# A pair of gate/up tiles, 2 of its 8 pairs of k tiles by seven products of block sums

## The reference

```python
x = _layer_norm(DEEPNORM_ALPHA * x + m, ln1_g, ln1_b)
x = _layer_norm(DEEPNORM_ALPHA * x + _swiglu(x, w_gate, w_up, w_down), ln2_g, ln2_b)
...
def _swiglu(x, w_gate, w_up, w_down):
    return (jax.nn.silu(x @ w_gate) * (x @ w_up)) @ w_down
```

## Time and profile before

| | |
|---|---|
| median of 3 runs | 953.99 us (953.26 to 954.17) |
| span of the profiled execution | 952.0 us |
| its time beside the span | the profiled execution has no time of its own on record; the median of the runs is 2.0 us above its span |
| TensorE busy | 99% of the span |
| DVE busy | 67% |
| ACT busy | 46% |
| GpSimd busy | 4% |
| loads | 192 GB/s over the span |

### The profile page before, as it was taken

One profiled execution on the slowest core, in us unless ns is written; L12 is line 12 of the kernel. 1 busy time (PEld: TensorE's weight loads), 2 busy tenths in 40 slices (PEclk: granted clock), 3 DMA queues, 4 the chain that ended last, 5 costly groups with the idle time before them and its releaser, 6 DMA issues.

```text
span 952.0 us, 12299 instructions
## 1 busy us (share of the span) xinstructions
PE 946.2 (99%) x4508; PEld 793.8 (83%) x4508; DVE 633.8 (67%) x1012; ACT 441.9 (46%) x573; POOL 40.9 (4%) x43
## 2 busy tenths in 40 slices
PE   9999999999999999999999999999999999999997
PEld 8999988888888888888888888888888888888885
DVE  6778566588776677777776776677775454554556
ACT  5676764362544444444444444444444343343450
POOL 0105530000000000000000000000000000000000
PEclk9999999999999999999999999999999999999999
DMA  9735225583365555554455555545457465464632
GB/s 365 318 140 177 97 82 185 209 347 142 108 219 204 180 203 190 186 209 178 176 184 211 204 193 185 210 178 194 181 209 291 141 232 188 160 237 156 225 129 88
DMA packets 28128, 183.57 MB, mean 193 GB/s; under 512 B 3136, under 2 KB 3648, under 8 KB 8640
## 3 DMA queue, kind: packets, MB, share of 16 engines
q1 hardware_dynamic: 28064, 183.12, 52.7%
q0 software_dynamic: 32, 0.00, 0.0%
HBM read 181.01 MB, written 2.10 MB: 192 GB/s over the span
## 4 chain that ended last, share of the span: by engine, by line
PE 99%; DVE 0%; ACT 0%; DVEq 0%; issue 0%; ACTq 0%
PE acc L1327 82%; PE acc L1265 5%; PE acc L1186 4%; PE acc L1464 2%; PE acc L1299 1%; PE tp L1378 1%; PE tp L1313 1%; PE tp L1391 1%; PE tp L1175 0%; PE tp L1404 0%; PE tp L1403 0%; PE tp L1402 0%; PE tp L1420 0%; PE acc L1555 0%; PE tp L1233 0%; DVE stats L1107 0%
## 5 line engine op out<-in xcount | busy, mean ns | idle before, releaser
L903 DVE TENSOR_TENSOR w_lo<-raw,w_hi 128x1024 fp32r<-128x1024 f32 (+1 forms) x283 | 335.3, 1194 | 242.4 <-ACT w_hi L627 240.6
L627 ACT ACTIVATE w_hi<-raw 128x1024 fp32r<-128x1024 f32 (+1 forms) x276 | 285.7, 1036 | 403.2 <-PE acc L1327 401.1
L1327 PE MATMUL acc<-w_hi,act_t 128*128 128x512 f32 x1344 | 413.9, 389 | 0.0
L1327 PEld LDWEIGHTS acc<-w_hi,act_t 128*128 128x128 f32 x1344 | 252.3, 188 | 52.5
L1327 PE MATMUL acc<-w_lo,act_t 128*128 128x512 f32 x672 | 261.4, 389 | 0.0
L1327 PE MATMUL acc<-w_hi,hid_t 128*128 128x512 f32 x672 | 207.2, 389 | 0.0
L1327 PEld LDWEIGHTS acc<-w_lo,act_t 128*128 128x128 f32 x672 | 126.1, 188 | 26.1
L1327 PEld LDWEIGHTS acc<-w_hi,hid_t 128*128 128x128 f32 x672 | 126.1, 188 | 26.1
L1327 PE MATMUL acc<-w_lo,hid_t 128*128 128x512 f32 x336 | 130.7, 389 | 0.0
L1047 DVE STREAM_TRANSPOSE turned<-hid 32x128 f32<-32x128 f32 x352 | 106.6, 303 | 5.6
L1327 PEld LDWEIGHTS acc<-w_lo,hid_t 128*128 128x128 f32 x336 | 63.1, 188 | 13.2
(11 more groups left out here) (179 smaller groups left out, 740.1 us busy)
## 6 DMA issues: line engine op xcount, KB each, us to landing
raw<-in_w_gu SPq DMA_DIRECT2D x88, 1024.0 KB, 4.8
raw<-in_w_down SPq DMA_DIRECT2D x32, 1024.0 KB, 4.6
raw<-in_w_out SPq DMA_DIRECT2D x16, 1024.0 KB, 4.8
raw<-in_w_down SPq DMA_DIRECT2D x16, 768.0 KB, 4.0
raw<-in_x_w SPq DMA_DIRECT2D x14, 552.0 KB, 7.1
raw<-in_w_uq SPq DMA_DIRECT2D x4, 1024.0 KB, 6.0
raw<-in_w_ukv SPq DMA_DIRECT2D x4, 1024.0 KB, 5.7
ln_rows<-in_ln_rows SPq DMA_DIRECT2D x4, 1024.0 KB, 7.3
```

Of the source, the lines that this page charges most:

```text
L627: act.activation(w_hi[:, (2 * slot + half) % RING, 0:n], raw[:, slot, first:first + n], ACT.Copy).then_inc(hi_done, 1)
L903: dve.tensor_tensor(w_lo[:, h, 0:n], raw[:, slot, first:first + n], w_hi[:, h, 0:n], ALU.subtract).then_inc(lo_done, 1)
L1327: last = pe.matmul(acc[:, bank0 + t, :], lhs[:, k, x, t * P:(t + 1) * P], part[:, w, n * GC:(n + 1) * GC], start=(start and x == 0 and par ...
```

## The change

Tiles 2 to 21 are taken in ten pairs (`pair(p)`: tiles 2p and 2p + 1). Of a pair's eight pairs of k tiles, the first two ("quads", q = 0 and 1) are multiplied in the way of Strassen and Winograd. For a quad, the activations are four blocks a11, a12, a21, a22 (token half by k tile) and the weights four blocks b11, b21, b12, b22 (k tile by tile of the pair), each 128 x 512; seven products of sums of blocks give what eight products of blocks gave. One split holds one factor for both quads, so it is followed by 2 x 3 = 6 matmuls into one bank. The other twelve k tiles are multiplied as before, six halves of 12 matmuls for the first tile of the pair and six for the second (`plain`).

- The sums of activations (s1 to s4) are made once by GpSimd beside tile 1, and split by ACT and GpSimd.
- Of the four sums of weights GpSimd makes b11 + b12 and b12 + b22, both in place in `raw`, from the time when DVE has made the low part of b11; DVE makes b11 + b22 (with the first sum in b11's place) and then b21's.
- ACT copies the partial result u from one bank to others, where further products are added to it (`seed`, three in a pair), and the product p5 to SBUF; DVE adds p5 to one bank and subtracts another from it.
- The work on finished tiles moves: the first tile of a pair has its `silu_step` and `gate_up` at plain half 9 and its transposes behind plain halves 0 and 1 of the next pair; the second tile's `gate_up` stands at plain half 2 of the next pair, and its transposes behind plain halves 3 and 4.
- `raw` has five slots, three for plain halves and two for quads. Tile 1 goes to banks of `tp`. The loops over tiles are written out.

```diff
+PAIRS = TILES // 2
+QUADS = 2
+PAIR_K = 2 * QUADS
+B11, B21, B12, B22 = range(4)
+S1, S2, S3, S4 = range(4)
+PRODUCTS = 7
+PLAIN = (KD - PAIR_K) // 2
+PAIR_HALVES = PRODUCTS + 2 * PLAIN
+PAIR_RING = 3
...
+        def used_pair(p, n):
+            base = USED_PAIRS + PAIR_SIGNALS * (p - 1)
+            if n in (PRODUCTS + PLAIN - 1, PAIR_HALVES - 1):
+                return ffn_full, 2 * p + (1 if n < PAIR_HALVES - 1 else 2)
+            return pe_used, base + n + (1 if n < PRODUCTS + PLAIN else 0)
+        def before_pair(p, n):
+            if n >= RING:
+                return used_pair(p, n - RING)
+            return used_ffn(1, TILE_HALVES - RING + n) if p == 1 else used_pair(p - 1, PAIR_HALVES - RING + n)
...
+        def banks_of(i):
+            if i == 0:
+                return acc[:, 0:2, :]
+            if i % 2 == 0:
+                return acc[:, 2:4, :]
+            return acc[:, 0:2, :] if i // 2 % 2 == 1 else tp[:, 0:2, :]
+        def quad(block):
+            return raw[:, PAIR_RING:PAIR_RING + QUADS, block * 512:(block + 1) * 512]
...
+            def load_quads(p):
+                if p > 1:
+                    sp.wait_ge(lo_done, v_pair(p - 1, PRODUCTS))
+                for q in range(QUADS):
+                    if p == 1 and q == 0:
+                        sp.wait_ge(lo_done, V_FFN + 2 * TILE_HALVES)
+                    sp.dma_start(raw[:, PAIR_RING + q, :],
+                                 w_pairs[p - 1][:, q * RAW_ELEMS:(q + 1) * RAW_ELEMS])\
+                      .then_inc(raw_full[PAIR_RING + q], 16)
...
+            def hi_product(p, n, block):
+                act.wait_ge(*before_pair(p, n))
+                act.activation(by_quad(w_hi[:, v_pair(p, n) % RING, :]), quad(block),
+                               ACT.Copy).then_inc(hi_done, 1)
...
+            def seed(p, n, dst, sign):
+                act.wait_ge(*used_pair(p, n))
+                act.activation(dst, banks_of(2 * p + 1)[:, 1, :], ACT.Copy, scale=sign).then_inc(seeded, 1)
+            def hi_pair(p):
+                first, second = banks_of(2 * p), banks_of(2 * p + 1)
+                for q in range(QUADS):
+                    act.wait_ge(raw_full[PAIR_RING + q], 16 * quad_fill(p, q))
+                hi_product(p, 0, B11)
+                act.wait_ge(t13_done, 2 * (p - 1) + 1)
+                hi_product(p, 1, B11)
+                act.wait_ge(t_done, 2 * (p - 1) + 1)
+                hi_product(p, 2, B11)
+                hi_product(p, 3, B21)
+                act.wait_ge(ffn_hid, 2 * p - 1)
+                seed(p, 0, first[:, 0, :], 1.0)
+                act.wait_ge(t13_done, 2 * p)
+                hi_product(p, 4, B12)
+                hi_product(p, 5, B22)
+                if p > 1:
+                    act.wait_ge(p5_added, 2 * (p - 1))
+                act.wait_ge(*used_pair(p, 1))
+                act.activation(p5_s[:], tp[:, 2, :], ACT.Copy).then_inc(p5_done, 1)
+                seed(p, 2, second[:, 0, :], -1.0)
+                act.wait_ge(t_done, 2 * p)
+                hi_product(p, 6, B21)
+                hi_plain(p, 0)
+                seed(p, 4, first[:, 1, :], 1.0)
+                for h in range(1, 2 * PLAIN):
+                    hi_plain(p, h)
+                    if h == 2 and p > 1:
+                        hid_hi(2 * p - 2)
+                    if h == 2:
+                        silu_step(2 * p - 1)
+                    if h == 6:
+                        hid_hi(2 * p - 1)
+                    if h == 9:
+                        silu_step(2 * p)
...
+            def lo_product(p, n, block):
+                v = v_pair(p, n)
+                dve.wait_ge(hi_done, v + 1)
+                dve.tensor_tensor(by_quad(w_lo[:, v % RING, :]), quad(block), by_quad(w_hi[:, v % RING, :]),
+                                  ALU.subtract).then_inc(lo_done, 1)
...
+            def t_sum(dst, x, y):
+                dve.tensor_tensor(quad(dst), quad(x), quad(y), ALU.add).then_inc(t_done, 1)
+            def lo_pair(p):
+                second = banks_of(2 * p + 1)
+                lo_product(p, 0, B11)
+                lo_product(p, 1, B11)
+                t_sum(B11, B11, B22)
+                lo_product(p, 2, B11)
+                lo_product(p, 3, B21)
+                t_sum(B21, B11, B21)
+                lo_product(p, 4, B12)
+                lo_product(p, 5, B22)
+                lo_product(p, 6, B21)
+                for h in range(2 * PLAIN):
+                    lo_plain(p, h)
+                    if h == 0 and p > 1:
+                        turn_hid(2 * p - 2, (0, 1))
+                    if h == 1 and p > 1:
+                        turn_hid(2 * p - 2, (2, 3))
+                    if h == 2:
+                        if p > 1:
+                            hid_lo(2 * p - 2)
+                        gate_up(2 * p - 1)
+                    if h == 3:
+                        turn_hid(2 * p - 1, (0, 1))
+                    if h == 4:
+                        turn_hid(2 * p - 1, (2, 3))
+                        dve.wait_ge(p5_done, p)
+                        dve.wait_ge(*used_pair(p, 5))
+                        dve.tensor_tensor(second[:, 0, :], p5_s[:], second[:, 0, :], ALU.add).then_inc(p5_added, 1)
+                        dve.wait_ge(seeded, 3 * p)
+                        dve.tensor_tensor(second[:, 1, :], p5_s[:], second[:, 1, :],
+                                          ALU.subtract).then_inc(p5_added, 1)
+                    if h == 6:
+                        hid_lo(2 * p - 1)
+                    if h == 9:
+                        gate_up(2 * p)
...
+            pool.wait_ge(xt_lo, TOK * CHUNKS)
+            first_k = act_t[:, 0:PAIR_K, :, :].rearrange("p (q k) x s -> p q k x s", q=QUADS)
+            pool.tensor_tensor(x1_t[:], first_k[:, :, :, 0, :], first_k[:, :, :, 1, :], ALU.add).then_inc(s_step, 1)
+            a11, a12 = x1_t[:, :, 0, 0:P], x1_t[:, :, 1, 0:P]
+            a21, a22 = x1_t[:, :, 0, P:S], x1_t[:, :, 1, P:S]
+            pool.wait_ge(s_step, 1)
+            pool.tensor_tensor(s_sum[:, S1, :, :], a21, a22, ALU.subtract).then_inc(s_step, 1)
+            pool.tensor_tensor(s_sum[:, S3, :, :], a11, a21, ALU.subtract).then_inc(s_step, 1)
+            pool.wait_ge(s_step, 3)
+            pool.tensor_tensor(s_sum[:, S2, :, :], s_sum[:, S1, :, :], a11, ALU.subtract).then_inc(s_step, 1)
+            pool.wait_ge(s_step, 4)
+            pool.tensor_tensor(s_sum[:, S4, :, :], a12, s_sum[:, S2, :, :], ALU.add).then_inc(s_step, 1)
+            pool.wait_ge(s_hi, 1)
+            pool.tensor_tensor(s_t[:, 1, :, :, :], s_sum[:], s_t[:, 0, :, :, :], ALU.subtract).then_inc(s_lo, 1)
+            for p in range(1, PAIRS):
+                pool.wait_ge(lo_done, v_pair(p, 0) + 1)
+                pool.tensor_tensor(quad(B11), quad(B11), quad(B12), ALU.add).then_inc(t13_done, 1)
+                pool.tensor_tensor(quad(B12), quad(B12), quad(B22), ALU.add).then_inc(t13_done, 1)
...
+            def strassen(p, n, what, out, start):
+                v = v_pair(p, n)
+                pe.wait_ge(lo_done, v + 1)
+                for q in range(QUADS):
+                    for x, part in ((0, w_hi), (0, w_lo), (1, w_hi)):
+                        last = pe.matmul(out, factor(q, what, x), part[:, v % RING, q * GC:(q + 1) * GC],
+                                         start=(start and (q, x) == (0, 0) and part is w_hi),
+                                         stop=((q, x) == (QUADS - 1, 1)), skip_group_check=not start)
+                last.then_inc(pe_used, 1)
+            def plain(p, h, out):
+                n = PRODUCTS + h
+                v, k0 = v_pair(p, n), PAIR_K + 2 * (h % PLAIN)
+                pe.wait_ge(lo_done, v + 1)
+                for m in range(2):
+                    for t in range(TOK):
+                        for x, part in ((0, w_hi), (0, w_lo), (1, w_hi)):
+                            last = pe.matmul(out[:, t, :], act_t[:, k0 + m, x, t * P:(t + 1) * P],
+                                             part[:, v % RING, m * GC:(m + 1) * GC], start=False,
+                                             stop=((h % PLAIN, m, x) == (PLAIN - 1, 1, 1)), skip_group_check=True)
+                last.then_inc(*((ffn_full, 1) if h % PLAIN == PLAIN - 1 else (pe_used, 1)))
+            def pair(p):
+                first, second = banks_of(2 * p), banks_of(2 * p + 1)
+                u, p5 = second[:, 1, :], tp[:, 2, :]
+                pe.wait_ge(ffn_hid, max(1, 2 * p - 2))
+                strassen(p, 0, "a11", u, True)
+                pe.wait_ge(s_lo, 1)
+                if p > 1:
+                    pe.wait_ge(p5_done, p - 1)
+                strassen(p, 1, "s1", p5, True)
+                pe.wait_ge(seeded, 3 * p - 2)
+                strassen(p, 2, "s2", u, False)
+                strassen(p, 3, "a12", first[:, 0, :], False)
+                pe.wait_ge(seeded, 3 * p - 1)
+                strassen(p, 4, "s3", u, False)
+                strassen(p, 5, "s4", second[:, 0, :], False)
```

(10 more changed lines are left out.)

224 lines of the change are left out of this document (160 added, 64 removed).

## The result

The changed kernel takes **1018.42 us** in the median (1015.35 to 1018.88, four runs), the kernel before 954.02 on the same chip: a ratio of 1.0672, 95% interval 1.0657 to 1.0687. The forecast was 1005.7 us with a range of 989 to 1017: the direction and most of the size were right, but the time was 12.7 us too low and lies above the range. The profiled execution is the one of 1015.35 us; the other three spanned some 3 us more.

The account below looks back on a forecast made before the run. TensorE was taken to bound the kernel. 9 x (5.1 + 1.1) + 8.8 + 0.7 - 13.6 = +51.7 us; with the 952.0 us span and 2.0 to the median, 1005.7 us, range 989 to 1017.

Parts of the forecast that it names:

- TensorE's saving of 13.6 us: In ten pairs, 42 product matmuls replace 48; 60 fewer at 0.2265 us give -13.6 us.
- The backlog, 5.1 us a pair: From product 2 to plain half 5, DVE's gapless 26.6 us outlasts TensorE's 20.4 us of work: +5.1 us a pair.
- near 90%: Expected sign in the profile: the share of a pair for which DVE is busy.
- GpSimd's second sum, 1.1 us a pair: Ahead of product 2, GpSimd's b12 + b22 holds DVE's low part of product 1: +1.1 us a pair.
- DVE goes first: Rival: GpSimd's second sum doesn't hold DVE's split; +40.7 us, 994.7 us in all; chance 0.30.
- the second sum is late: Rival: DVE stops GpSimd altogether, so product 4's split waits for the second sum; 1014.7 us; chance 0.13.
- a share of 88%: At product 1, the later of DVE and GpSimd loses 88% of the shared time, here of 1.25 us.
- The first pair, 8.8 us: Late quad loads and the chain of sums and splits delay the first pair's products: +8.8 us.
- lie beside tile 1 ... and cost nothing: GpSimd's activation sums, under 10 us of tile 1's 21.75, were to cost nothing.
- the 6.5 assumed: Landing time in us taken for the first pair's two quad loads, between 4.8 and 7.3.
- The down start, 0.7 us: At the down stage's start, transposes of two tiles beside halves of 12 and 6 matmuls: +0.7 us.
- The clock: TensorE expected at 2.4 GHz throughout; rival with falls to 1.2 GHz: 1055 us, chance 0.08 shared with a slow sum.

Follow-up runs that it names:

- e7: Changed kernel with DVE's transposes spread over later plain halves and all four weight sums on DVE; 953.51 us, ratio 0.9994.
- e1: Changed kernel with the transposes, gate_up and hid_lo spread over the plain halves, same instructions; 973.17 us, ratio 1.0211.
- e2: Changed kernel with GpSimd's second weight sum (b12 + b22) given to DVE ahead of product 1's low part; 1005.03 us, ratio 1.0539.
- e12: e10 with the last activation sum a half earlier on ACT and GpSimd, and without GpSimd's wait for hid_lo of tile 0; 943.36 us.
- e10: e7 with the first pair's quads loaded a tile earlier, into tile 0's place, and GpSimd's last activation sum behind hid_lo of tile 0; 943.74 us.
- e6: Changed kernel with GpSimd's last activation sum behind tile 1's splits and the first pair's two quad loads exchanged; 1014.61 us, ratio 1.0638.
- e5: Changed kernel with eight spare matmuls into an unread bank ahead of plain half 5 of each pair; 1014.57 us, ratio 1.0638.
- e9: e3 with eight spare matmuls into an unread bank ahead of plain half 5 of each pair; 991.06 us, ratio 1.0394.
- e4: Changed kernel with GpSimd's second weight sum made to wait for DVE's b11 + b22; 1020.63 us, ratio 1.0698.
- e3: Changed kernel with all four weight sums on DVE, none on GpSimd; 1004.53 us, ratio 1.054.

## Why the prediction was wrong, and where it was right

*TensorE's saving of 13.6 us*: right. e7's step of 42.16 us is 1.34 below the 43.5 of before, and the products run with six matmuls into one bank at no loss.

*The backlog, 5.1 us a pair*: right. DVE's stretch was 26.7 us for 26.6. The undisturbed step, less e7's 42.16 and the 1.1 of the hold, leaves 5.2. e1 removed 4.25 of it by order alone, while the same work stayed on DVE: what counts is the place, as the prediction said. One sign was misstated: DVE is busy for 39.0 of the 48.48 us of that pair, 80% and not "near 90%"; the prediction's own 37.9 of 48.3 is 78%.

*GpSimd's second sum, 1.1 us a pair*: right in size (1.09 in the trace, 1.04 by e2), and the rivals "DVE goes first" and "the second sum is late" are out. How it comes about was only half right: it isn't a share of 88%. In places of different overlap, the later instruction is longer by what is left of the earlier one, less 0.13 or 0.14: 0.68 left give 0.54 (246.48, tile 1), 1.23 give 1.09 (469.12), 2.35 give 2.22 (hid_lo), 2.33 give 2.19 (e12), 2.34 give 2.20 (e10). It holds the other way round too: GpSimd's 3.25 in e10 is 2.40 and the 0.99 that DVE's split of 261.42 had left, less 0.14. The Trainium skill, "SBUF — State Buffer", section "Who interferes with whom", says that the later one is blocked until the first ends. The traces agree: the 0.14 can be read as the later instruction's own start, which the block doesn't lengthen. With a large overlap it matters which of the two one uses. The prediction says that no trace of the kernel before shows DVE as the later one; it does. Beside GpSimd's masks, two of DVE's low parts of 1104 columns, 1.31 us alone (22.94), take 1.40 and 1.50 with 0.24 and 0.34 us of GpSimd's instruction left (25.38 and 26.70): about the same rule, and enough to doubt "DVE goes first" before any run. It isn't without exception: a split at 89.73 keeps its 1.23 with 0.58 us of a GpSimd scaling left, which the runs don't explain.

*The first pair, 8.8 us*: the mechanism was right, the size wrong; product 2 is 12.4 us late and product 4 13.0 (it starts at 287.16 and was due four products, 5.44 us, behind 268.7). The first step of the prediction that failed is that GpSimd's sums of activations "lie beside tile 1 ... and cost nothing". They hold DVE twice. The first five hold its splits at the start of tile 1, and with them all that follows: 1.4 us. The last one holds hid_lo, and with it tile 1's last low part, for which the quads wait: 2.2 us. e6 shows the second; the first is read from the trace, and no run takes it away. The quads take 7.1 us from issue to ACT (264.91 to 271.98) for the 6.5 assumed. These make the 4.2 us.

*The down start, 0.7 us*: right. The down stage's 1056 matmuls take 240.3 us (from 765.35) for 239.5 before (from 704.62), 0.8 more; the one idle time that the profile lists there (0.28, ahead of 776.89) is only a part of it, as the matmul ahead is counted busy for 0.39 us where it would be followed after 0.23.

*The clock*: wrong, and the other half of the error. This is the second step that failed, a term put at nothing: the prediction expected "2.4 GHz throughout", as TensorE stood near idle for 5 us at the end of the kernel at a granted 1.00. That row is a mean over 52 us, in which the start of a fall doesn't show: from 951.0 to 951.9 the granted clock of the same trace is 0.95, and no matmul ran behind it that could have shown the price. In the changed kernel the clock goes to 1.2 GHz at the first pair and behind the wait ahead of plain half 5 in three of nine pairs, 1.64 us each, 4.9 in all. e5 and e9 show that this wait is the cause: filled with spare matmuls, none of the sixteen steps is long. But it is no sufficient cause: with waits of the same 2.1 us the clock fell in 3 of 9 pairs in the changed kernel, in e2 and in e6, in 4 in e4 and in 8 in e3. What decides, the runs leave open.

The sum for the profiled execution: the prediction's 1003.7 of span, and 4.2 (first pair), 9 x 0.13 = 1.2 (steady pairs), 4.9 (clock) and 0.1 (down start), less the 0.7 by which TensorE reached tile 1 earlier than in the profile before, give 1013.4 of the 1013.6 measured. The other three executions span 3.2 us more with a mean clock of 0.987 for 0.990. Two more falls would be 3.3; there is no trace of them, so that is argued and not shown.

## What to carry to other kernels

When work is taken from the bounding engine, walk the next engine's queue over the shortened stretch and not over the period: DVE had 38 us of work for 42, and still cost 5 us a pair until its transposes stood elsewhere. Price a two-input instruction on DVE beside one on GpSimd at the whole rest of the earlier one, also where GpSimd's work seems to be off the path: what it holds may be what a load waits for, even through a chain of instructions that follow each other without a gap. And a new wait of about 2 us on TensorE may cost 1.6 us more by the clock; filling it with spare matmuls is free where the wait is real, and costs their time where it isn't.

## What the runs showed that I had not expected

- DVE and GpSimd, each with two SBUF inputs, exclude each other both ways: the later is longer by the rest of the earlier, less 0.14 us (0.54, 1.09, 2.19, 2.20 and 2.22 us longer on DVE, 0.85 on GpSimd). At the start of tile 1 they take turns: GpSimd's sum ends at 247.15, DVE's split at 248.23, the next sum at 248.83, the next split at 249.91.
- TensorE's clock fell to 1.2 GHz behind waits of 2.1 us in a kernel that keeps TensorE busy for 94% of the span, for 1.64 us a time, and in 3 or 8 of 9 like places.
- Exchanging the two loads of the first pair gained nothing, though one was issued 2.5 us ahead of the other: ACT waits for both, and its first split came 1.93 us earlier (270.05 instead of 271.98), no more than the 2.2 that hid_lo alone gave back.
